# A decoder step on one core: the prompt group's final retention state computed and stored in the routing stretch instead of among the branch projections

## The chip, the core and the metric

One Trainium2 core runs the whole program. The metric is device time in microseconds (us) of one execution. The kernel before took 1251.85, 1258.98 and 1262.05 us in three runs, median 1258.98 us. One execution was also profiled, and its trace is what this document reads.

## What is computed

264 tokens (256 of a prompt, 8 decode samples) go through one layer: an input projection, three token mixers (a recurrent branch, a retention branch, cross attention to memory), a gated merge, an output projection, and then a mixture of 32 experts with a router. The change touches one output of the retention branch alone, the state that the prompt leaves behind (`ret_p`, 4 heads x 256 x 512, 2 MB in float32):

```
def step(s, inp):                       # retention, per chunk and head
    qc, kc, vc = inp
    att = einsum('bhnk,bhmk->bhnm', qc, kc) * dmask
    o = einsum('bhnm,bhmv->bhnv', att, vc) + einsum('bhnk,bhkv->bhnv', qc * q_decay, s)
    s = s * s_decay + einsum('bhmk,bhmv->bhkv', kc * k_decay, vc)
    return s, o
s_last, o = lax.scan(step, s0, chunks)  # s_last of the prompt group is ret_p
...
grp_logits = x @ w_grp + b_grp          # router: top group, then 2 of its 8 experts
y = sum over experts of (silu(x @ w_gate) * (x @ w_up) * weight) @ w_down
```

For the prompt, which starts from a zero state, `s_last` is one product per head, decayed keys transposed times values over all 256 positions. Nothing later in the layer reads it: it only has to be stored.

## The kernel before

Activations lie transposed, channels on the 128 partitions and the 264 tokens along the free axis. All engines follow one list of tasks that `tensor_order` writes out (line 250 on), each taking from it the tasks it has a part in, in that order. TensorE (PE) makes a product into one of eight PSUM banks, ScalarE (ACT) or VectorE (DVE) takes it out. Projections (`ga`, `gc`, `lru_out`, `mem_out`, ...: 128 output channels each, 8 products of 128x128 by 128x264) turn over banks 0 to 3, side tasks over banks 4 to 6. PE waits at a task for its bank (`begin`), the evicting engine for the product (`full`).

**The branch stretch.** `tensor_order` weaves 32 projections with the prompt's retention tasks `ret` (per head: `att`, four `o`, and two `S`) and with the tasks of the 16 half states of the samples (`sd`, `so`: 8 samples x 2 pairs of heads, 1 MB each, in a ring of three buffers `st`). A half state goes through four engines: POOL loads it (line 895), ACT decays it in two halves (`sd`, copies of 128x1024 with a scale), DVE adds key times value (`sd`, line 1654, four instructions), PE reads it with the query (`so`, line 1193), and POOL stores it (line 920). POOL's loop per half state is: wait for the update, store, copy a row of values to partition 0 with a small DMA (line 901), wait for that, broadcast the row (line 905), load the half state after next. Task `S` is what the change moves: `("S", h, i)` is two products of 128x128 by 128x512 (line 1181, `k_rows` and `v_rows`), a copy by ACT into one of two buffers `S_st`, and a 256 KB store to `ret_p` issued from ACT's queue (line 1376). ACT waits for the store before last before it fills a buffer again.

**After it** come the last projections (`gb`, `g`, `ret_out`, `x2`) and the normed residual, which ends the list.

**The routing stretch.** `router_products` (line 605 on) has PE make the router's logits (line 609), transpose the tokens back to rows in six steps u = 0 to 5 (line 618; u = 4 and 5 are the last 8 tokens), and, when DVE has the expert masks, the ranks of the tokens (lines 631 to 634). ACT copies each step's rows out in two forms and then a middle part (loop at 1411 to 1427), POOL makes the remainders. Behind the copies of u = 2 ACT waits for DVE (`router_exp_in`) and takes an exponential that DVE waits for. DVE picks groups and experts in a chain of small instructions up to the masks (line 1770), then waits for the ranks. `gather(0, 0)` (line 648) starts the expert loop on PE: 16 pairs of experts, whose weights SP streams, 12 MB a pair. SP's queue in this stretch holds the weights of expert 1 (line 795), four parts of the last expert that have a buffer of their own (`last_gate_up`, line 798), and then the loop's loads, each waiting until PE is through with the buffer (line 809).

Buffers are placed by lifetimes in stages (`BUFFERS`: size, first stage, last stage).

Of the kernel before, what the change touches and what calls it, by code (L numbers as in the profile page):

```python
# [33 lines left out]
P = 128  # L34
D = 1024
# [27 lines left out]
def shape_constants():  # L63
# [85 lines left out]
    "vT": (VT * T, "v", "rows"),  # L149
    "v_rows": (2 * HEADS * DV, "rows", "gc"),  # L150
    "k_rows": (2 * D, "v", "gc"),
    "vs_rows": (HEADS * DV, "rows", "gc"),
# [8 lines left out]
    "oT": (VT * T, "ga", "ret"),  # L161
    "S_st": (2 * DV, "ga", "gb"),
    "os": (DV, "ga", "gb"),
# [6 lines left out]
    "rbias": (NLOG, "load", "end"),  # L170
    "last_gate_up": (4 * CHUNK, "x2", "end"),
    "filler": (24, "route", "end"),
# [76 lines left out]
def tensor_order():  # L249
# [29 lines left out]
    for h in heads:  # L279
        ret += [("att", h)] + [("o", h, j) for j in range(4)] + [("S", h, i) for i in range(2)]  # L280

# [51 lines left out]
def build_program(nc, dram, outs, const_at):  # L333
# [55 lines left out]
    with ExitStack() as ctx:  # L389
# [156 lines left out]
        st_decayed, st_updated, st_read = sem("st_decayed"), sem("st_updated"), sem("st_read")  # L546
        s_out = [sem("s_out_0"), sem("s_out_1")]
        o_normed, g_tanh, ret_ready = sem("o_normed"), sem("g_tanh"), sem("ret_ready")
        branch_merged = sem("branch_merged")
# [20 lines left out]
        def states_stored(eng):  # L570

            for i in range(3):
                eng.wait_ge(st_out[i], 16 * len(range(i, 2 * NS, 3)))
            for i in range(2):
                eng.wait_ge(s_out[i], 16 * HEADS)

# [26 lines left out]


        def router_products(pe):

# [4 lines left out]
            for u in range(2 * TT):  # L611
                t, k4 = divmod(u, 2)
                n = min(P, T - t * P)
                if u >= 2:

                    pe.wait_ge(row_high, u - 1)
                for k in range(4):
                    mm = pe.transpose(psum[0:n, u % 2, k * P:(k + 1) * P], xnT[:, 4 * k4 + k, t * P:t * P + n], ident)
                mm.then_inc(row_full, 1)
                if u == 1:  # L620
                    pe.wait_ge(logitsT_ready, 1)
                    for s in range(TT):
                        m = min(P, T - s * P)
                        mm = pe.transpose(psum[0:m, 2, s * 64:s * 64 + NLOG], lgT[0:NLOG, s * P:s * P + m],
                                          ident[0:NLOG, 0:NLOG])
                    mm.then_inc(logits_full, 1)
            pe.wait_ge(masks_ready, 1)
            pe.wait_ge(tables_set, 2)
# [114 lines left out]
        def _(sp):  # L743
# [48 lines left out]
            for i in range(6):  # L792
                if i < RING1:
                    full(sp, last_task[max(n for n in range(NCH) if n % RING1 == i)])
                sp.dma_start(into(i, i), expert_part(1, i)).then_inc(chunk_loaded[i], 16)

            for i in range(4):
                sp.dma_start(last_gate_up[:, i, :].rearrange("p (k n) -> p k n", k=4),
# [30 lines left out]
            for q in range(4):  # L829
                sp.wait_ge(final_normed, 2 * q + 2)  # L830
                sp.dma_start(outs["y"].rearrange("(k p) n -> p k n", p=P)[:, 2 * q:2 * q + 2],
                             y_out[:, 2 * q:2 * q + 2]).then_inc(stored, 16)
            sp.wait_ge(stored, 16 * 4)
            sp.nop()
# [126 lines left out]
        def _(pe):  # L961
# [56 lines left out]
            for task in order:  # L1018
# [146 lines left out]
                elif kind == "o":  # L1165
                    _, h, j = task
                    if j == 0:
# [6 lines left out]
                                        start=False, stop=True))  # L1174
                elif kind == "S":
                    _, h, i = task
                    if i == 0:
                        read(pe, ("kr", 1, 1))
                    begin(task)
                    for m in range(2):  # L1180
                        mm = pe.matmul(ps(task)[:, 0:DV], k_rows[:, m, (2 * h + i) * P:(2 * h + i + 1) * P],  # L1181
                                       v_rows[:, m, h * DV:(h + 1) * DV], start=m == 0, stop=m == 1)
                    end(task, mm)
                elif kind == "so":
# [51 lines left out]
        def _(act):  # L1236
# [12 lines left out]
            for task in order:  # L1249
# [114 lines left out]
                elif kind == "o":  # L1364
                    _, h, j = task
                    full(act, task)
                    run(oT[:, 4 * h + j, 0:TP], ps(task)[:, 0:TP], ACT.Copy, free_of(task))
                elif kind == "S":
                    _, h, i = task
                    n = 2 * h + i  # L1370
                    full(act, task)
                    if n >= 2:
                        act.wait_ge(s_out[n % 2], 16 * (n // 2))
                    run(S_st[:, n % 2, :], ps(task), ACT.Copy, free_of(task))
                    steps.settle()
                    act.dma_start(outs["ret_p"][h, i * P:(i + 1) * P, :], S_st[:, n % 2, :]).then_inc(s_out[n % 2], 16)
                elif kind == "oq":
# [29 lines left out]
            def rows_of(u):  # L1407
                t, k4 = divmod(u, 2)
                return min(P, T - t * P), t, slice(512 * k4, 512 * k4 + 512)

            for u in range(2 * TT + 1):
                if u < 2 * TT:
# [12 lines left out]
                if u == 2:  # L1425
                    act.wait_ge(router_exp_in, 1)
                    run(tmpB[:, 0:TT * 8], tmpB[:, 0:TT * 8], ACT.Exp, router_exp)

            def take_tokens(g, half):
# [47 lines left out]
        def _(dve):  # L1477
# [17 lines left out]
            for task in order:  # L1495
# [100 lines left out]
                elif kind in ("rot_q", "rot_k"):  # L1596
# [5 lines left out]

                    full(dve, ("i", KT - 1))
                    v(V.tensor_tensor(t1, x2_, sin, ALU.mult))
# [9 lines left out]
                elif kind == "sl":  # L1614

                    full(dve, ("i", KT - 1))
                    v(V.memset(buf("PM"), 0.0))
# [303 lines left out]
```

## Time and profile before

| | |
|---|---|
| three runs | 1251.85, 1258.98, 1262.05 us |
| span of the profiled execution | 1255.6 us |
| busy PE / DVE / ACT / POOL | 1185.2 / 385.5 / 237.3 / 100.3 us |
| share of the chain that ended last, by engine | PE 89%, DVE 6%, ACT 2%, DMA 1% |
| branch stretch, `sd`/`so` tasks | 335 to 508 us |
| routing stretch, last `x2` product to first gather | 685 to 722 us |
| expert pairs | 722 to 1243 us |

Times in rows are us from the start of the span. "L1181" is line 1181 of the kernel before. ACT's evictions all carry L1240, the line of a helper, so they are told apart by shape and time. A float32 product counts as two instructions of PE. The granted TensorE clock (PEclk) stands as a share of full speed: 1.00 is 2.4 GHz, 0.50 is 1.2 GHz.

### The profile page before, as it was taken

Reading aid. Unit: us, or ns where it says so; the run is one execution under the profiler, and the core shown is the slowest. Engines: PE = TensorE matmul, PEld = TensorE weight load, DVE = VectorE, ACT = ScalarE, POOL = GpSimd, SP = SyncE. Lnnn points to the kernel's source line nnn. Section 1 sums busy time; section 2 is a strip of 40 time slices with the busy share of each in tenths; the row PEclk is TensorE's granted clock in tenths of the full one; section 3 lists DMA queues with packets and bytes.
Section 4 is the critical chain, followed back from the end, with each engine's and each line's share of the span. In section 5 each row is a group of like instructions: output and inputs, shape, how many; then the busy total and the mean of one; then the engine's idle time right before and its main releaser. Section 6 shows DMA issues by size and latency. Waiting matters only on the chain.

```text
span 1255.6 us, 18012 instructions
## 1 busy us (share of the span) xinstructions
PE 1185.2 (94%) x7398; PEld 776.4 (62%) x7398; DVE 385.5 (31%) x696; ACT 237.3 (19%) x449; POOL 100.3 (8%) x127
## 2 busy tenths in 40 slices
PE   6999999999889999999998399999999999999996
PEld 5888888778666766888887154444444444444442
DVE  1203572385323334232111752222211222222222
ACT  2112124123422222321001311111111111111112
POOL 0001120000332322000000400000000000000000
PEclk9999999999999999999999689999999999999999
DMA  8774566675688889335356738999999999999981
GB/s 282 241 256 143 171 210 225 195 244 136 215 273 310 293 279 307 127 126 185 103 167 241 292 135 313 394 394 394 394 394 395 394 394 394 394 394 394 394 310 37
DMA packets 187948, 343.36 MB, mean 273 GB/s; under 512 B 7640, under 2 KB 91864, under 8 KB 187896
## 3 DMA queue, kind: packets, MB, share of 16 engines
q1 hardware_dynamic: 172288, 287.95, 64.2%
q0 software_dynamic: 14464, 52.68, 12.2%
q10 hardware_dynamic: 1152, 2.10, 0.4%
q8 instruction: 33, 0.54, 0.2%
q14 instruction: 11, 0.09, 0.0%
HBM read 320.47 MB, written 22.20 MB: 273 GB/s over the span
## 4 chain that ended last, share of the span: by engine, by line
PE 89%; DVE 6%; ACT 2%; DMA 1%; issue 1%; POOL 0%; DVEq 0%; ACTq 0%
PE psum L988 35%; PE psum L686 18%; PE psum L710 9%; PE psum L648 6%; PE psum L1038 4%; PE psum L723 4%; PE psum L1193 2%; PE psum L997 2%; ACT arena L1240 2%; DVE arena L1808 2%; PE psum L1007 1%; PE psum L1181 1%; DVE arena L1553 1%; DMA arena<-arena 1%; PE psum L1132 1%
## 5 line engine op out<-in xcount | busy, mean ns | idle before, releaser
L988 PE MATMUL psum<-arena 128*128 128x264 f32 x2048 | 473.4, 388 | 0.0
L988 PEld LDWEIGHTS psum<-arena 128*128 128x128 f32 x2048 | 386.1, 190 | 82.2 <-issue 18.6
L1240 ACT ACTIVATE arena<-psum 128x256 f32<-128x256 f32 (+3 forms) x276 | 117.9, 442 | 632.4 <-PE psum L988 263.2
L686 PE MATMUL psum<-arena 128*64 128x512 f32 x1024 | 228.9, 598 | 0.9 <-ACT arena L1240 0.9
L686 PEld LDWEIGHTS psum<-arena 128*64 128x64 f32 x1024 | 73.4, 138 | 141.7 <-issue 141.6
L710 PE MATMUL psum<-arena 128*64 128x512 f32 x512 | 113.4, 595 | 11.1 <-ACT arena L1240 11.1
L1801 DVE SCALAR_TENSOR_TENSOR arena<-arena,psum 128x256 f32<-128x256 f32 x32 | 13.5, 422 | 346.4 <-ACT arena L1240 346.4
L648 PEld LDWEIGHTS psum<-arena 128*128 128x128 bf16 x2304 | 70.7, 99 | 28.0 <-issue 28.0
L1654 DVE SCALAR_TENSOR_TENSOR arena<-arena 128x512 f32<-128x512 f32 x64 | 54.8, 916 | 105.5 <-ACT arena L1240 90.4
L1240 ACT ACTIVATE arena<-arena 128x1024 f32<-128x1024 f32 (+7 forms) x67 | 58.7, 903 | 150.6 <-DVE arena L1694 84.8
L710 PEld LDWEIGHTS psum<-arena 128*64 128x64 f32 x512 | 35.3, 137 | 78.9 <-issue 64.0
L723 PE MATMUL psum<-arena 128*128 128x264 f32 x272 | 78.4, 411 | 5.2 <-ACT arena L1455 1.3
L648 PE MATMUL psum<-arena 128*128 128x64 bf16 x2304 | 74.5, 195 | 2.7 <-DVE arena L1795 2.7
L1808 DVE TENSOR_TENSOR arena<-arena,psum 128x264 f32<-128x264 f32 x136 | 58.3, 429 | 52.5 <-PE psum L723 51.4
L723 PEld LDWEIGHTS psum<-arena 128*128 128x128 f32 x272 | 42.0, 188 | 35.8 <-DVE arena L1808 25.2
L1038 PE MATMUL psum<-arena 128*128 128x256 f32 x256 | 56.3, 379 | 3.1 <-DVE arena L1501 3.1
L1038 PEld LDWEIGHTS psum<-arena 128*128 128x128 f32 x256 | 48.2, 190 | 9.8 <-issue 3.4
L1455 ACT ACTIVATE arena<-psum 128x1024 f32<-128x1024 f32 x16 | 16.4, 1024 | 115.9 <-PE psum L710 115.9
L1193 PE MATMUL psum<-arena 128*8 128x512 f32 x128 | 30.2, 593 | 3.2 <-DVE arena L1654 3.2
L905 POOL PARTITION_BROADCAST arena<-arena x16 | 21.8, 1360 | 106.6 <-DMA arena<-arena 106.6
L997 PE MATMUL psum<-arena 128*128 128x264 f32 x128 | 29.8, 386 | 0.0
L997 PEld LDWEIGHTS psum<-arena 128*128 128x128 f32 x128 | 24.3, 190 | 4.2
(233 smaller groups left out, 641.5 us busy)
## 6 DMA issues: line engine op xcount, KB each, us to landing
arena<-in_w_gate SPq DMA_DIRECT2D x64, 1024.0 KB, 13.5
arena<-in_w_up SPq DMA_DIRECT2D x64, 1024.0 KB, 14.1
arena<-in_w_down SPq DMA_DIRECT2D x64, 1024.0 KB, 12.8
arena<-in_w_in SPq DMA_DIRECT2D x48, 1024.0 KB, 5.3
arena<-in_state_ret POOLq DMA_DIRECT2D x16, 1024.0 KB, 6.8
out_ret_s<-arena POOLq DMA_DIRECT2D x16, 1024.0 KB, 7.6
arena<-in_w_mem_kv SPq DMA_DIRECT2D x8, 1024.0 KB, 9.5
arena<-in_cache_mem_k POOLq DMA_DIRECT2D x8, 1024.0 KB, 5.9
```

The lines of the kernel that those rows point to most:

```text
L648: mm = pe.matmul(psum[:, 0, k * SLOTS:(k + 1) * SLOTS], xr[x][:, t, k * P:(k + 1) * P], Sb[:, t, half * SLOTS:(half + 1) * SLOTS], start=t ...
L686: mm = pe.matmul(psum[64 * a:64 * a + SLOTS, 2, :], XgT[:, half, k, :], w[:, :, 256 * a:256 * a + 256], start=k == 0, stop=k == KT - 1)
L710: mm = pe.matmul(psum[64 * half:64 * half + SLOTS, 4 + dh, :], hT[:, half, f % 2, f // 2, :], w[:, f % 2, dh * 512:(dh + 1) * 512], start= ...
L723: pe.matmul(psum[:, 6 + d % 2, 0:T], yS[:, d * P:(d + 1) * P], SwT, start=True, stop=True).then_inc(scatter_full, 1)
L905: nc.gpsimd.partition_broadcast(vb[:, s % 2, :], v_row0[0:1, :], P).then_inc(v_bcast, 1)
L988: mm = pe.matmul(ps(task)[:, 0:T], w[:, k, (i % 2) * P:(i % 2 + 1) * P], rhs[:, k, :], start=k == 0, stop=k == KT - 1 and not two)
L997: mm = pe.matmul(ps(task)[:, 0:T], w[:, k, (i % 2) * P:(i % 2 + 1) * P], rhs[:, KT + k, :], start=False, stop=k == KT - 1)
L1038: mm = pe.matmul(ps(task)[:, 0:256], memT[:, k, m * P:(m + 1) * P], w[:, k, :], start=k == 0, stop=k == KT - 1)
L1193: mm = pe.matmul(psum[32 * h:32 * h + NS, 7, :], QM[:, 2 * h + i, b, :], st[:, s % 3, 2 * h2 + i, :], start=b == 0 and i == 0, stop=b == N ...
L1240: steps.did(nc.scalar.activation(out, in_, func, **kw), sem)
L1654: did(V.scalar_tensor_tensor(x, vb[:, s % 2, h2 * DV:(h2 + 1) * DV], kT[:, 2 * (2 * hp + h2) + i, TP + b:TP + b + 1], x, ALU.mult, ALU.add ...
L1808: V.tensor_tensor(x_res[:, d, :], x_res[:, d, :], psum[:, 6 + d % 2, 0:T], ALU.add).then_inc(scatter_added, 1)
```

## The change

Task `S` leaves the woven list. Its products become `state_products`, called from `router_products` behind the transposes of u = 2 (state 0), 3 (state 1), 4 (states 2 and 3) and 5 (states 4 to 7), into banks 4 and 5. Its copies and stores become `stage_states`, called in ACT's loop over u at u = 3 (state 0), 4 (1), 5 (2 and 3) and 6 (4 to 7). PE waits at state n for the copy of state n - 2, ACT from state 2 on for the store of state n - 2. `k_rows` and `v_rows` now live until the routing stretch, `last_gate_up` only from the expert loop on, and SP loads it when all eight products are done. The waits on all of `ret_p`'s stores go to the end of SP's program. At two places DVE waits for ACT's eviction of the last `i` gate where it waited for PE's product.

```diff
-    "v_rows": (2 * HEADS * DV, "rows", "gc"),
-    "k_rows": (2 * D, "v", "gc"),
+    "v_rows": (2 * HEADS * DV, "rows", "route"),
+    "k_rows": (2 * D, "v", "route"),
...
-    "S_st": (2 * DV, "ga", "gb"),
+    "S_st": (2 * DV, "route", "route"),
...
-    "last_gate_up": (4 * CHUNK, "x2", "end"),
+    "last_gate_up": (4 * CHUNK, "moe", "end"),
...
-        ret += [("att", h)] + [("o", h, j) for j in range(4)] + [("S", h, i) for i in range(2)]
+        ret += [("att", h)] + [("o", h, j) for j in range(4)]
...
-            for i in range(2):
-                eng.wait_ge(s_out[i], 16 * HEADS)
...
+        def state_products(pe, states):
+            for n in states:
+                h, i = divmod(n, 2)
+                if n == 0:
+                    read(pe, ("kr", 1, 1))
+                if n >= 2:
+                    pe.wait_ge(s_staged, n - 1)
+                for m in range(2):
+                    mm = pe.matmul(psum[:, 4 + n % 2, :], k_rows[:, m, (2 * h + i) * P:(2 * h + i + 1) * P],
+                                   v_rows[:, m, h * DV:(h + 1) * DV], start=m == 0, stop=m == 1)
+                mm.then_inc(s_full, 1)
...
                     mm.then_inc(logits_full, 1)
+                if u >= 2:
+                    state_products(pe, ((), (), (0,), (1,), (2, 3), (4, 5, 6, 7))[u])
             pe.wait_ge(masks_ready, 1)
...
+            sp.wait_ge(s_full, 2 * HEADS)
             for i in range(4):
                 sp.dma_start(last_gate_up[:, i, :].rearrange("p (k n) -> p k n", k=4),
...
+            for i in range(2):
+                sp.wait_ge(s_out[i], 16 * HEADS)
             sp.wait_ge(stored, 16 * 4)
...
-                elif kind == "S":
-                    _, h, i = task
-                    n = 2 * h + i
-                    full(act, task)
-                    if n >= 2:
-                        act.wait_ge(s_out[n % 2], 16 * (n // 2))
-                    run(S_st[:, n % 2, :], ps(task), ACT.Copy, free_of(task))
-                    steps.settle()
-                    act.dma_start(outs["ret_p"][h, i * P:(i + 1) * P, :], S_st[:, n % 2, :]).then_inc(s_out[n % 2], 16)
...
+            def stage_states(states):
+                for n in states:
+                    h, i = divmod(n, 2)
+                    act.wait_ge(s_full, n + 1)
+                    if n >= 2:
+                        act.wait_ge(s_out[n % 2], 16 * (n // 2))
+                    run(S_st[:, n % 2, :], psum[:, 4 + n % 2, :], ACT.Copy, s_staged)
+                    act.wait_ge(s_staged, n + 1)
+                    act.dma_start(outs["ret_p"][h, i * P:(i + 1) * P, :], S_st[:, n % 2, :]).then_inc(s_out[n % 2], 16)
...
+                if u >= 3:
+                    stage_states(((0,), (1,), (2, 3), (4, 5, 6, 7))[u - 3])
...
-                    full(dve, ("i", KT - 1))
+                    read(dve, ("i", KT - 1))
```

The end of the branch stretch on PE, before. L1181 is task `S`, L1193 `so`, L988 a projection, L1172 and L1173 task `o`; the last L1193 reads half state 15.

```order
L1193 MATMUL psum<-arena 8x512 x4
L988 MATMUL psum<-arena 128x264 x8
L1172 MATMUL psum<-arena 128x256
L1173 MATMUL psum<-arena 128x128
L988 MATMUL psum<-arena 128x264 x8
L1181 MATMUL psum<-arena 128x512 x2
L1193 MATMUL psum<-arena 8x512 x4
L988 MATMUL psum<-arena 128x264 x8
L1181 MATMUL psum<-arena 128x512 x2
L1193 MATMUL psum<-arena 8x512 x4
L988 MATMUL psum<-arena 128x264 x16
```

The same place with the change. `so` is L1201, a projection L1005, task `o` L1189 and L1190.

```order
L1201 MATMUL psum<-arena 8x512 x4
L1005 MATMUL psum<-arena 128x264 x8
L1189 MATMUL psum<-arena 128x256
L1190 MATMUL psum<-arena 128x128
L1005 MATMUL psum<-arena 128x264 x8
L1201 MATMUL psum<-arena 8x512 x4
L1005 MATMUL psum<-arena 128x264 x8
L1189 MATMUL psum<-arena 128x256
L1190 MATMUL psum<-arena 128x128
L1201 MATMUL psum<-arena 8x512 x4
L1005 MATMUL psum<-arena 128x264 x16
```

The two `S` are gone; between the last two `so` stand one projection and one `o`.

PE in the routing stretch with the change, from the transposes of u = 4 (first row) to the ranks (last row). L613 is a state product; each waits for a copy by ACT (`s_staged`).

```order
L630 MATMUL psum<-arena 8x128 [waits row_high]
L630 MATMUL psum<-arena 8x128 x3
L613 MATMUL psum<-arena 128x512 [waits s_staged]
L613 MATMUL psum<-arena 128x512
L613 MATMUL psum<-arena 128x512 [waits s_staged]
L613 MATMUL psum<-arena 128x512
L630 MATMUL psum<-arena 8x128 [waits row_high]
L630 MATMUL psum<-arena 8x128 x3
L613 MATMUL psum<-arena 128x512 [waits s_staged]
L613 MATMUL psum<-arena 128x512
...
L646 MATMUL psum<-arena 128x32 [waits tables_set,masks_ready]
```

Before, the L613 rows were not there: the ranks stood directly behind the eight transposes of u = 4 and 5. Three more states (5 to 7) stand where the line of dots is.

ACT in the same stretch with the change, from the exponential to the copy of state 2. The rows of 8x512 are the row copies of u = 4 and u = 5.

```order
L1248 ACTIVATE arena<-arena 128x24 [waits router_exp_in]
L1248 ACTIVATE arena<-psum 128x512 [waits row_rest,row_full]
L1248 ACTIVATE arena<-psum 128x512
L1248 ACTIVATE arena<-arena 128x512 [waits row_rest]
L1248 ACTIVATE arena<-psum 128x512 [waits s_full]
L1419 DMA out_ret_p<-arena 128x512 [waits s_staged]
L1248 ACTIVATE arena<-psum 8x512 [waits row_rest,rows_zero,row_full]
...
L1248 ACTIVATE arena<-psum 8x512 [waits row_rest,row_full]
L1248 ACTIVATE arena<-psum 8x512
L1248 ACTIVATE arena<-arena 8x512 [waits row_rest]
L1248 ACTIVATE arena<-psum 128x512 [waits s_out_0,s_full]
```

Before, the rows that wait for `s_full` and the stores (L1419) were not there. State 0 is copied behind the exponential, and state 2 behind the row copies of u = 5, which wait for PE's transposes (`row_full`).

## Rows read from the trace of the kernel before

**Rows 1.** The page: span.
```profile
span 1255.6 us, 18012 instructions
```

**Rows 2.** Busy time by stretch: PE, PEld, DVE, ACT, POOL, PEclk, DMA share, GB/s.
```profile
335.00:508.00 173.00, 169.33 (x731) 117.94 (x730) 63.23 (x87) 42.81 (x65) 47.84 (x58) 0.99 0.82 278
...
697.00:722.00 25.00, 5.01 (x41) 3.04 (x41) 21.60 (x54) 10.85 (x20) 14.79 (x17) 0.63 0.71 268
```

**Rows 3.** Chain that ended last, end of the branch stretch: start, us, what.
```profile
497.30 1.72 PE psum L1181 x4
499.02 1.82 PE psum L1193 x8
```

**Rows 4.** Waits of PE, ACT and POOL, 335 to 510: us in total, times, longest.
```profile
PE psum L1172 <- DVE arena L1644: 3.7, 1, 3.7
...
ACT arena L1240 <- DMA arena<-in_state_ret: 52.2, 13, 8.9
...
POOL arena L905 <- DMA arena<-arena: 97.7, 15, 8.5
POOL out_ret_s L920 <- DVE arena L1654: 19.8, 10, 7.6
```

**Rows 5.** Timeline, POOL: first and last of 13 state loads: start, us, instruction.
```profile
350.68 0.82 POOL L895 DMA_DIRECT2D arena<-in_state_ret  x1
...
486.57 0.80 POOL L895 DMA_DIRECT2D arena<-in_state_ret  x1
```

**Rows 6.** Timeline: decay and update of half state 15 [idle before, releaser].
```profile
492.22 2.00 ACT L1240 ACTIVATE arena<-arena 128x1024 f32<-128x1024 f32 x2 [5.36 <-DMA arena<-in_state_ret]
...
494.37 2.74 DVE L1654 SCALAR_TENSOR_TENSOR arena<-arena 128x512 f32<-128x512 f32 x4 [4.83 <-ACT arena L1240]
```

**Rows 7.** DMA, 335 to 510 (packets, MB, share; issues); last row whole span.
```profile
q10 hardware_dynamic: 1152, 2.10, 3.1%
...
out_ret_p<-arena ACTq DMA_DIRECT2D x8, 256.0 KB, 4.8
...
out_y<-arena SPq DMA_DIRECT2D x4, 264.0 KB, 2.2
```

**Rows 8.** Timeline, ACT: copy and store of one state in the branch stretch.
```profile
350.98 0.60 ACT L1240 ACTIVATE arena<-psum 128x512 f32<-128x512 f32 x1 [1.32 <-PE psum L1181]
351.61 0.40 ACTq L1376 DMA_DIRECT2D out_ret_p<-arena  x1
```

**Rows 9.** Timeline of the routing stretch: u = 3 and 5, and the ranks.
```profile
709.20 1.07 ACT L1240 ACTIVATE arena<-psum 128x512 f32<-128x512 f32 x2
...
710.15 0.63 ACT L1240 ACTIVATE arena<-arena 128x512 bf16<-128x512 f32 x1
...
710.32 1.02 PE L618 MATMUL psum<-arena 128*8 128x128 f32 x4 [6.85 <-ACT arena L1240]
...
718.67 0.21 PE L632 MATMUL psum<-arena 128*128 128x32 bf16 x1 [7.34 <-DVE arena L1770]
```

**Rows 10.** Busy time in steps of 5 us, columns as in Rows 2.
```profile
705.00:710.00 5.00, 0.00 (x0) 0.00 (x0) 3.99 (x20) 0.93 (x3) 0.85 (x1) 0.50 1.05 387
...
715.00:720.00 5.00, 0.42 (x9) 0.32 (x9) 4.65 (x11) 0.63 (x1) 4.66 (x9) 0.50 0.00 0
```

**Rows 11.** Chain that ended last, first expert pair: gathers and gate-up products.
```profile
721.83 4.01 PE psum L648 x72
...
726.71 9.03 PE psum L686 x32
735.74 2.21 PE psum L648 x72
...
743.36 7.02 PE psum L686 x32
```

**Rows 12.** Timeline, SP: the expert loop's first load.
```profile
732.49 0.39 SPq L809 DMA_DIRECT2D arena<-in_w_gate  x1
```

**Rows 13.** Timeline, DVE: first instruction that needs the gate bank's successor (task `sl`).
```profile
220.43 0.41 DVE L1621 TENSOR_REDUCE arena<-psum 32x1 f32<-32x256 f32 x1 [2.49 <-PE psum L1114]
```

More of the change, by code:

```diff
@@ L547, in build_program @@
         s_out = [sem("s_out_0"), sem("s_out_1")]
+        s_full, s_staged = sem("s_full"), sem("s_staged")
         o_normed, g_tanh, ret_ready = sem("o_normed"), sem("g_tanh"), sem("ret_ready")
@@ L1174, in _ @@
                                         start=False, stop=True))
-                elif kind == "S":
-                    _, h, i = task
[L1177 to L1183, printed above, removed]
                 elif kind == "so":
@@ L1367, in _ @@
                     run(oT[:, 4 * h + j, 0:TP], ps(task)[:, 0:TP], ACT.Copy, free_of(task))
-                elif kind == "S":
-                    _, h, i = task
-                    n = 2 * h + i
-                    full(act, task)
-                    if n >= 2:
-                        act.wait_ge(s_out[n % 2], 16 * (n // 2))
-                    run(S_st[:, n % 2, :], ps(task), ACT.Copy, free_of(task))
-                    steps.settle()
-                    act.dma_start(outs["ret_p"][h, i * P:(i + 1) * P, :], S_st[:, n % 2, :]).then_inc(s_out[n % 2], 16)
                 elif kind == "oq":
@@ L1614, in _ @@
                 elif kind == "sl":
-                    full(dve, ("i", KT - 1))
+                    read(dve, ("i", KT - 1))
                     v(V.memset(buf("PM"), 0.0))
```

## Prediction

> **What bounds the kernel now.** I read the shares of the chain first: PE is 89% of it, so whatever leaves PE looks like a gain. The question is stretch by stretch whether PE's work there, or something PE is about to wait for, ends last.
>
> In the branch stretch PE is busy 169.3 of 173 us at a granted clock of 0.99 [rows 2], and it stands still once, 3.7 us [rows 4]. That reads as bound by PE. But a second chain runs beside it, the 16 half states of the samples, and the waits say that it does not depend on PE: ACT waits 13 times for a half state to land, POOL 15 times for the small row DMA (97.7 us) and 10 times for DVE's update (19.8 us), and neither POOL nor DVE's updates wait for PE [rows 4]. POOL issues the last 13 loads from 350.68 to 486.57 us, one in 11.3 us [rows 5]. The last half state is decayed as it lands (492.22) and its update ends at 494.37 + 2.74 = 497.1 [rows 6]; PE reads it at 499.02, right behind the last `S` [rows 3]. So at the end of this stretch PE is only 1.9 us behind the state chain. Two bounds lie almost on each other.
>
> In the routing stretch PE works 5 of 25 us, with the clock at 0.63 [rows 2]. There DVE's mask chain sets the end: PE waits 7.34 us for it before the ranks at 718.67 [rows 9], and the gather follows at 721.83 [rows 11]. ACT works 10.85 of the 25 us and POOL 14.79 [rows 2].
>
> **The change part by part.**
>
> *Removed from the branch stretch:* 8 tasks `S`, 16 products. A pair takes 1.72 us on PE at full clock [rows 3], together 13.8 us. Each also takes a copy of 0.60 us and a store issue of 0.40 us on ACT [rows 8], 8 us, which lie in ACT's waiting time. What PE gains it loses again waiting for the half states: without `S`, PE is ready for the last `so` some 12 us early, but the update still ends at 497.1. The last `so` therefore starts at about 497.2 instead of 499.02: 1.8 us. Two order rows show what is left between the last two `so`, one projection and one `o`, which is not enough to make PE late again.
>
> The state chain itself may get a little faster, since the stores to `ret_p` leave the DMA engines: they took 3.1% of the 16 engines' time in this window [rows 7], 5.4 us. Nothing of it is gained if the chain's waits are for its own transfers, all of it if every store stood in the chain's way. The row DMA stands behind a store and beside a load of 1 MB each on its own queue, against which 256 KB are small; I take 1.5 us. Branch stretch: -3.3 us (-1.8 to -7.2).
>
> *The 3.7 us stall* at an `o` is on PE alone. With the change more such stalls come, up to some 12 us in all; they cost nothing as long as the state chain ends last.
>
> *Added to the routing stretch.* On PE 8 pairs, chained with ACT's copies by `s_staged`, and ACT's copies chained with the stores from state 2 on. All of PE's part stands ahead of the ranks in PE's order. I follow it in the times of the trace.
> - States 0 and 1 go behind the transposes of u = 2 and 3, before ACT's exponential; PE waits there anyway. Free.
> - ACT copies state 0 only behind the exponential and the work of u = 3: copies from 709.20 (1.07), middle part (0.63, from 710.15) [rows 9], copy 0.60 [rows 8]: 711.3. Only then may PE start state 2.
> - PE has idled for 6.85 us at that time, and the clock stands at 0.50 from 705 on [rows 10]: a pair takes 3.44 us instead of 1.72. States 2 and 3: 711.3 + 6.9 = 718.2 (state 1 is copied at 713.7, in time). The transposes of u = 5, which in the kernel before ran at 710.32, follow: 1.02 us [rows 9], 719.2.
> - ACT is waiting for those: copies 1.07, middle part 0.63, copy of state 2 0.60: 721.5. Store issue 0.40, copy of state 3: 722.5.
> - PE, states 4 and 5: I take full clock. In the first pair PE began at 721.83, and its 9.03 us of gate-up products are 4.0 us at half and 5.0 at full clock if 7.02 is the whole at full clock [rows 11], so the clock rose at about 730.7, behind 8.9 us of work; here PE has by 721.5 worked for 10 us with one gap. 721.5 + 3.4 = 724.9.
> - State 4 is copied when the store of state 2 has landed. A 264 KB store into idle engines took 2.2 us [rows 7], and here they are idle, at share 0.00 from 715 to 720 [rows 10]: 723.7, copied 724.3; state 5, with its product at 724.9: 725.5.
> - States 6 and 7: 724.9 to 728.4. The ranks follow there instead of at 718.67: +9.7 us.
>
> What is queued behind: on PE the ranks, for which DVE waits with the slots, and so the gather and all 16 pairs; on ACT only the copy of the first gather, later than the copy of state 7; on SP `last_gate_up` and the loop's first load.
>
> Bounds: all pairs at full clock, state 2 on, moves everything from u = 5 on 3.3 us earlier: +6.4. All at half clock: 721.5 + 4 x 3.44 = 735.3, +16.6. Stores as slow as in the branch stretch, 4.8 us [rows 7]: states 4 and 5 copied at 726.9 and 727.9, last product at 730.3, +11.6.
>
> The Trainium skill ("DMA: Bandwidth & Descriptors", section "Issuing engines are not separate DMA queues") says that transfers issued by ACT run on the same 16 engines as those of SP and interleave with them; weights under way here would give the +11.6. The trace speaks for idle engines, as the row of 715 to 720 shows.
>
> *Given back.* In the kernel before the first gather and the first gate-up products come on a cold PE: 4.01 and 9.03 us against 2.21 and 7.02 in the next half pair [rows 11]. If the state products keep the clock up across the 3 us from ranks to gather, 3.8 us come back; if it falls again, none. I take half, 1.9. Routing stretch: +7.8 us (+2.6 to +16.6).
>
> *`last_gate_up` later.* Four loads of 1 MB at 387 GB/s [rows 10] are 10.8 us. They leave when all products are done, 3.4 us before the gather; the loop's first load comes 10.7 us behind the gather [rows 11, 12], so there are 14 us for them. Cost 0; without that cover, up to 10.8.
>
> *The two waits on the gate's eviction, and the lifetimes:* DVE's two memsets start one eviction later, under 1 us, and DVE idles 2.49 us behind them before the next instruction, for PE [rows 13]. Cost 0. The waits at the end cost 0, the stores are over 500 us old.
>
> **Sum.** -3.3 + 7.8 = +4.5 us. The profiled span is 1255.6 [rows 1]; the median of the runs, 1259.0, lies 3.4 us above, within the spread of the three. I add the change to the median: 1263.5 us.
>
> **The rivals.**
> 1. *The clock stays at 0.50 throughout the routing stretch* (slower). PE's pairs come in bursts between waits for ACT. Then +16.6, nothing given back, and with the smallest branch gain, -1.8, the sum is +14.8: 1273.8. For it: the rows of 705 to 720 stand at 0.50. Against it: from 711.3 on PE has work with gaps of some 2 us only. It decides from the third state on: pairs of states 4 to 7 at 3.4 us instead of 1.7. The Trainium skill ("TensorE: Matmul & The Clock Gate", section "Part 1: The HAM clock gate") calls the throttled clock the default that activity releases. By it work moved from a busy stretch into an idle one costs double, which speaks against this change; the two levels stand in the rows, 0.99 in the branch stretch and 0.50 here. Chance 0.15.
> 2. *The branch stretch really is bound by PE* and gives all 13.8 us: -13.8 + 7.8 = -6.0, 1253.0; with the cheapest routing stretch (+2.6) -11.2, 1247.8. For it: PE's busy share. Against it: POOL, ACT and DVE show no wait for PE in the state chain. It would need half states at 10.5 us apiece instead of 11.3. Chance 0.12.
> 3. *`last_gate_up` pushes the loop's loads* and the first pairs wait for weights: up to 10.8 us on top of +4.5, 1274.3. Against it: the 14 us of cover. Chance 0.05.
> 4. My forecast, 1254.4 (-7.2 + 2.6) to 1268.8 (-1.8 + 11.6): chance 0.68.
>
> **Range and chances.** From 1251 to 1274: it leaves out the better part of rival 2 and the worst of rivals 1 and 3. A measurement of this kernel tells about 1%, 12.6 us, from no change. Slower by over 1% is most of rival 1, part of rival 3 and the tip of the forecast with a bad draw: 0.17. Faster by over 1% is rival 2 at its best: 0.05. Within 1%: 0.78.
>
> **What would show it.** Right: the last `so` starts only 2 to 7 us earlier, and PE now waits for DVE's updates at most `so`; the state loads still come every 11 us; PE waits for ACT's copies at the state products from state 2 on; the ranks come 8 to 12 us later after the last `x2`; the first gather takes nearer 2.2 than 4.0 us. Wrong: branch stretch shorter by over 8 us; the state products done before DVE's masks; weights late in pair 1; or states 4 to 7 on a half clock.

## The result, and the profile after

Over 20 runs of each kernel the median went from 1259.53 to 1268.87 us. The ratio is 1.0057, with a 95% interval from 1.0032 to 1.0082: the change costs 7.2 us (4.0 to 10.3). (The medians lie 9.3 us apart; the ratio leaves out runs over 1.5% above the fastest of their kernel.) It is a small loss, but the interval leaves no doubt of its sign, which the forecast of +4.5 us had right.

The profiled execution of the changed kernel spans 1265.1 us, against 1255.6 [rows 1]. A second execution of each was profiled later, with no edit, because the first pair differs in two places and one of them turned out to be chance. They are called "again" below. Times are from the start of the span; the last column is the span less the column before it.

| | last state updated | first router product | exponential | ranks | second gate-up | span | rest |
|---|---|---|---|---|---|---|---|
| before | 497.1 | 690.47 | 709.07 | 718.67 | 743.29 | 1255.6 | 512.3 |
| before again | 497.9 | 689.74 | 706.51 | 716.11 | 740.92 | 1253.4 | 512.5 |
| after | 504.0 | 695.54 | 712.38 | 732.18 | 752.82 | 1265.1 | 512.3 |
| after again | 497.5 | 690.59 | 707.70 | 725.37 | 747.39 | 1259.6 | 512.2 |

Three things can be read here. Behind the second gate-up products nothing changed. From the exponential on, the changed kernel is 6.2 us longer in the first pair (40.44 against 34.22) and 5.3 us in the second (39.69 against 34.41). The end of the branch stretch is 7 us later in the first pair and as good as equal in the second.

**The branch stretch.** Busy time of the changed kernel, columns as in [rows 2]:

```profile
335.00:508.00 173.00, 155.15 (x674) 109.00 (x674) 58.58 (x85) 37.67 (x57) 48.86 (x58) 0.94 0.78 261
```

PE's busy time in this window fell from 169.33 [rows 2] to 155.15 us, by about the 13.8 us of the eight `S`. The stretch got no shorter for it. PE now stands still for 17.9 us instead of 3.7, and the waits from 335 to 510 us (total, times, longest) say for whom:

```profile
POOL arena L922 <- DMA arena<-arena: 106.5, 15, 9.4
ACT arena L1248 <- DMA arena<-in_state_ret: 101.6, 13, 12.1
...
PE psum L1189 <- DVE arena L1656: 11.6, 2, 5.9
...
PE psum L1201 <- DVE arena L1666: 6.3, 2, 4.9
```

POOL still waits 15 times for its small row DMA, and ACT 13 times for a half state, now 101.6 instead of 52.2 us [rows 4]. Decay, update and query of half state 15, in the timeline (start, duration, instruction, idle before and releaser):

```profile
499.09 2.00 ACT L1248 ACTIVATE arena<-arena 128x1024 f32<-128x1024 f32 x2 [5.79 <-DMA arena<-in_state_ret]
...
501.23 2.74 DVE L1666 SCALAR_TENSOR_TENSOR arena<-arena 128x512 f32<-128x512 f32 x4 [6.47 <-ACT arena L1248]
...
504.03 1.89 PE L1201 MATMUL psum<-arena 128*8 128x512 f32 x8 [1.36 <-DVE arena L1666]
```

Here the order is plain: the state lands, ACT, DVE, and PE takes it 0.06 us after the update ends. Before, the last `so` came 1.9 us after it, behind an `S` [rows 3, 6]. In after again PE came to the last `so` at 499.07, 1.6 us behind the update and without a wait: there it had lost its time earlier, 13.9 us over the stretch.

**The routing stretch.** The same view of the changed kernel:

```profile
695.54 5.44 PE L621 MATMUL psum<-arena 128*36 128x264 f32 x16 [3.51 <-DVE arena L1713]
...
712.38 0.22 ACT L1248 ACTIVATE arena<-arena 128x24 f32<-128x24 f32 x1 [2.70 <-DVE arena L1767]
...
714.63 6.37 PE L613 MATMUL psum<-arena 128*128 128x512 f32 x8 [6.12 <-ACT arena L1248]
720.84 0.60 PE L630 MATMUL psum<-arena 128*8 128x128 f32 x4
...
723.59 8.75 PE L613 MATMUL psum<-arena 128*128 128x512 f32 x16 [2.15 <-ACT arena L1248]
...
727.23 0.60 ACT L1248 ACTIVATE arena<-psum 128x512 f32<-128x512 f32 x1 [1.58 <-PE psum L613]
...
732.18 0.18 PE L646 MATMUL psum<-arena 128*128 128x32 bf16 x1
732.37 0.37 SPq L813 DMA_DIRECT2D arena<-in_w_gate  x1
...
734.98 2.26 PE L662 MATMUL psum<-arena 128*128 128x64 bf16 x72 [2.42 <-DVE arena L1807]
738.12 7.09 PE L700 MATMUL psum<-arena 128*64 128x512 f32 x32 [0.88 <-ACT arena L1248]
```

PE idles 6.12 us until ACT, behind the exponential, has copied state 0. Then states 2 and 3 take 6.37 us where 3.44 would do at full clock, PE waits 2.15 us for ACT again, and states 4 to 7 take 8.75 us. The ranks no longer wait for DVE's masks, as they did for 7.34 us [rows 9]: they have no bracket, PE simply gets to them last. In return the first gather takes 2.26 and its gate-up products 7.09 us, where it was 4.01 and 9.03 [rows 11].

The clock in this place (columns as in [rows 2]):

```profile
710.00:715.00 5.00, 0.37 (x1) 0.37 (x2) 4.16 (x15) 2.20 (x5) 2.24 (x3) 0.50 0.00 0
715.00:720.00 5.00, 5.00 (x7) 1.90 (x7) 4.65 (x11) 2.06 (x4) 3.17 (x3) 0.50 0.28 105
720.00:725.00 5.00, 2.85 (x9) 1.36 (x8) 0.27 (x2) 2.65 (x5) 2.25 (x2) 0.84 0.11 44
725.00:730.00 5.00, 5.00 (x10) 2.00 (x9) 0.00 (x0) 1.82 (x3) 2.40 (x6) 0.81 0.30 113
```

From 715 to 720 PE is busy all the time and is granted 0.50, 1.2 GHz: the engine had idled for 6.12 us just before. In the kernel before PE did 0.42 us of work there [rows 10]. In the last two rows the clock is at 1.00 from 720 on, falls to 0.50 once more at the start of states 4 to 7, behind the pause of 2.15 us (hence the means of 0.84 and 0.81), and stands at 1.00 from 727 on, the gather included. In after again it stayed at 1.00 across that same pause, so that states 4 to 7 took 7.13 us, and fell in the pause ahead of the gather, which took 3.71 us.

### The profile page after: what moved, and what is told of

Its sections match the earlier page's. It is cut to its first block, busy times and chain, and to the rows that moved or that the text cites. A ratio compares the mean times of both kernels' runs of the same rounds, so it can differ in the third digit from the quotient of the medians.

```text
span 1265.1 us, 18004 instructions
## 1 busy us (share of the span) xinstructions
PE 1189.0 (94%) x7398; PEld 777.4 (61%) x7398; DVE 378.6 (30%) x696; ACT 236.5 (19%) x449; POOL 101.9 (8%) x127
## 4 chain that ended last, share of the span: by engine, by line
PE 76%; DVE 7%; issue 6%; DMA 4%; ACT 3%; POOL 2%; DVEq 0%; POOLq 0%; ACTq 0%
PE psum L1005 26%; PE psum L700 17%; PE psum L724 9%; PE psum L662 5%; PE psum L1055 4%; PE psum L737 4%; ACT arena L1248 3%; DMA arena<-in_state_ret 3%; PE psum L1014 2%; DVE arena L1820 2%; DVE arena L1666 1%; DMA arena<-arena 1%; PE psum L1024 1%; POOL arena L922 1%; PE psum L613 1%
## 5 line engine op out<-in xcount | busy, mean ns | idle before, releaser
L1005 PE MATMUL psum<-arena 128*128 128x264 f32 x2048 | 473.9, 388 | 0.0
L1005 PEld LDWEIGHTS psum<-arena 128*128 128x128 f32 x2048 | 387.1, 191 | 82.1 <-issue 18.0
L1248 ACT ACTIVATE arena<-psum 128x256 f32<-128x256 f32 (+4 forms) x276 | 117.4, 441 | 596.4 <-PE psum L1005 244.3
L1248 ACT ACTIVATE arena<-arena 128x1024 f32<-128x1024 f32 (+7 forms) x67 | 58.7, 903 | 197.4 <-DMA arena<-in_state_ret 101.6
L1666 DVE SCALAR_TENSOR_TENSOR arena<-arena 128x512 f32<-128x512 f32 x64 | 51.1, 859 | 122.1 <-ACT arena L1248 107.4
L1820 DVE TENSOR_TENSOR arena<-arena,psum 128x264 f32<-128x264 f32 x136 | 58.2, 429 | 51.2 <-PE psum L737 50.1
L737 PEld LDWEIGHTS psum<-arena 128*128 128x128 f32 x272 | 42.1, 188 | 35.9 <-DVE arena L1820 26.4
L1201 PE MATMUL psum<-arena 128*8 128x512 f32 x128 | 32.8, 637 | 9.6 <-DVE arena L1666 9.6
## 6 DMA issues: line engine op xcount, KB each, us to landing
arena<-in_w_up SPq DMA_DIRECT2D x64, 1024.0 KB, 14.1
```

Of the source, the lines that this page charges most:

```text
L737: pe.matmul(psum[:, 6 + d % 2, 0:T], yS[:, d * P:(d + 1) * P], SwT, start=True, stop=True).then_inc(scatter_full, 1)
L1005: mm = pe.matmul(ps(task)[:, 0:T], w[:, k, (i % 2) * P:(i % 2 + 1) * P], rhs[:, k, :], start=k == 0, stop=k == KT - 1 and not two)
L1201: mm = pe.matmul(psum[32 * h:32 * h + NS, 7, :], QM[:, 2 * h + i, b, :], st[:, s % 3, 2 * h2 + i, :], start=b == 0 and i == 0, stop=b == N ...
L1248: steps.did(nc.scalar.activation(out, in_, func, **kw), sem)
L1666: did(V.scalar_tensor_tensor(x, vb[:, s % 2, h2 * DV:(h2 + 1) * DV], kT[:, 2 * (2 * hp + h2) + i, TP + b:TP + b + 1], x, ALU.mult, ALU.add ...
L1820: V.tensor_tensor(x_res[:, d, :], x_res[:, d, :], psum[:, 6 + d % 2, 0:T], ALU.add).then_inc(scatter_added, 1)
```

## The experiments

Each ratio is against runs of the kernel before on the same chip. The theory: in the branch stretch the chain of half states ends last, so `S` is free there; in the routing stretch the states' products and copies, chained between PE and ACT, delay the ranks. The rivals: PE bounds the branch stretch; the products alone, or the clock, make the routing stretch dear.

**1. No `S` at all** (`ret_p` is not computed or stored; compared with the kernel before).

```diff
-        ret += [("att", h)] + [("o", h, j) for j in range(4)] + [("S", h, i) for i in range(2)]
+        ret += [("att", h)] + [("o", h, j) for j in range(4)]
...
-            for i in range(2):
-                eng.wait_ge(s_out[i], 16 * HEADS)
```

> The kernel before with task S left out altogether (ret_p is not computed, 8 pairs of products, 8 copies and 8 stores fewer, nothing put in their place). It measures what the branch stretch gives back when S leaves. Theory A, the half states' chain (load, decay, update, store, row DMA) ends that stretch: within -3 to +4 us of the kernel before, although 13.8 us of products at full clock are gone, and PE waits for DVE's updates at most `so`. Rival, PE bounds the stretch: -13.8 us, ratio about 0.989.

1261.44 against 1258.14 us, ratio 1.0001 (0.9967 to 1.0035, which is -4.2 to +4.4 us). 13.8 us of PE's work, eight copies and eight stores less make no difference. That PE alone bounds the branch stretch is excluded; so is a relief of the state chain through the missing stores of more than some 4 us. The waits of this kernel in the branch stretch show where the time went:

```profile
POOL arena L903 <- DMA arena<-arena: 109.7, 15, 10.6
...
PE psum L1191 <- DVE arena L1652: 9.0, 4, 3.5
...
PE psum L1170 <- DVE arena L1642: 7.9, 2, 5.1
```

PE waits for DVE at four of the sixteen `so` (L1191), not at most of them as expected, and at two `o` (L1170), and POOL for its row DMA no less than before.

**2. The same load on PE in the routing stretch, tied to nothing** (the kernel before with eight pairs of products of the same shape, on data that lies there anyway, no copies and no stores).

```diff
                     mm.then_inc(logits_full, 1)
+                if u >= 3:
+                    for n in range((2, 2, 4)[u - 3]):
+                        for m in range(2):
+                            pe.matmul(psum[:, 4 + n % 2, :], ident, buf("x")[:, 512 * m:512 * m + 512],
+                                      start=m == 0, stop=m == 1)
```

> The kernel before with 8 pairs of 128x128 by 128x512 products added on PE in the routing stretch, behind the transposes of u = 3 (2), 4 (2) and 5 (4), read by nobody and waiting for nobody. It measures the clock term alone: products there without copies and stores. If they end before the masks (718.7 us) and keep the clock at 2.4 GHz, the first gather falls from 4.0 to 2.2 us and the first gate-up products from 9.0 to 7.0: -3.8 us in all. If the products run at 1.2 GHz throughout, the last four end some 5 us behind the masks and the sum is +1 to +5 us.

1259.18 us, ratio 0.9995 (0.9962 to 1.0028). From the first router product to the ranks 26.2 us, as in before again (26.4). So PE's work alone costs nothing that could be measured in this place (-4.8 to +3.5 us). The timeline, from the last four pairs on:

```profile
724.19 7.03 PE L630 MATMUL psum<-arena 128*128 128x512 f32 x16
...
732.12 0.19 PE L637 MATMUL psum<-arena 128*128 128x32 bf16 x1 [0.90 <-DVE arena L1775]
...
735.28 3.34 PE L653 MATMUL psum<-arena 128*128 128x64 bf16 x72 [2.77 <-DVE arena L1800]
739.50 8.77 PE L691 MATMUL psum<-arena 128*64 128x512 f32 x32 [0.88 <-ACT arena L1245]
```

The four pairs ran at full clock (7.03 us), PE then waited 0.90 us for the masks instead of 7.3, and still the gather and the gate-up products were slow. The expected gain of 3.8 us came to about 1 in this trace (23.7 us from the ranks to the second gate-up, against 24.6 and 24.8 before). A warm PE at the ranks does not secure the clock behind them.

**3. Both kernels again, profiled only.**

> The changed kernel once more, for a second execution's trace. If the state chain of the branch stretch ended late in the first trace (update of half state 15 at 504.0 us against 497.1 before) because of the change, it is again at 502 to 506 here; if that was one execution's draw of DMA times, it lies anywhere from 495 to 506. The routing stretch is the same to within 1 us: ranks 42 us behind the last x2 product.

> The kernel before once more, for a second execution's trace: if the end of its state chain (497.1 us in the first) is a draw, it moves by several us here; if it is set by the program, it is within 1 us.

1261.24 and 1255.22 us. The numbers stand in the table above. In after again the last update came at 497.5, which by the expectation makes the 504.0 a draw. In before again it moved by 0.8 us only, which by itself would have said that the program sets it; experiment 2 says otherwise. The ranks came 42.0 us behind the last `x2` products in after and 40.2 in after again, so the routing stretch was not the same to within 1 us. The update of half state 15 in after again, in before again, and in experiment 2, whose branch stretch is the program of before:

```profile
494.72 2.74 DVE L1666 SCALAR_TENSOR_TENSOR arena<-arena 128x512 f32<-128x512 f32 x4 [4.26 <-ACT arena L1248]
```
```profile
495.13 2.74 DVE L1654 SCALAR_TENSOR_TENSOR arena<-arena 128x512 f32<-128x512 f32 x4 [5.09 <-ACT arena L1240]
```
```profile
506.95 2.74 DVE L1659 SCALAR_TENSOR_TENSOR arena<-arena 128x512 f32<-128x512 f32 x4 [4.73 <-ACT arena L1245]
```

With `S` in the stretch the last update ended at 497.1, 497.9 and 509.7 us, without it at 504.0, 497.5, 504.7 (experiment 1) and 502.3 (experiment 6). The spread from execution to execution, 12 us, is larger than the 7 us of the first pair, which must not be read as the effect of the change.

**4. Before, with POOL's row DMA issued ahead of the store.** In the kernel before POOL stores a half state and only then fetches the next row of values, on the same queue. Here the row (and the load of a half state) goes first:

```diff
                 b, hp = n_state(s)
+                if s + 2 < 2 * NS:
+                    v_row(s + 2)
+                    if s >= 1:
+                        load_state(s + 2)
                 pool.wait_ge(st_updated, s + 1)
...
                 if s + 2 < 2 * NS:
-                    v_broadcast(s + 2)
-                    if s >= 1:
-                        load_state(s + 2)
+                    v_spread(s + 2)
```

> The kernel before with another order in POOL's loop over the half states: row DMA and next load are issued ahead of the wait for the update and of the store, and the broadcast comes behind the store. Theory A (half states and PE bound the branch stretch almost equally before): the state chain gets shorter, but PE's work including S then bounds alone, so only the stall at one `o` and the last wait go: 0 to -6 us, and the last update ends well ahead of the last `so`. If the chain were bound by DMA bandwidth and not by the order, nothing changes.

1252.07 against 1260.61 us, ratio 0.9931 (0.9906 to 0.9955): 8.7 us (5.7 to 11.9), more than the 0 to 6 expected. The expectation counted the 3.7 us for which PE stood still in one execution; in before again it was 0.9, and in experiment 2, whose branch stretch is the same program, 14.1. The waits and the busy time of the branch stretch in this kernel:

```profile
POOL arena L895 <- DMA out_ret_s<-arena: 92.6, 13, 9.3
...
POOL arena L911 <- DMA arena<-arena: 4.9, 2, 4.1
```
```profile
335.00:508.00 173.00, 172.73 (x754) 120.82 (x752) 54.66 (x91) 44.71 (x69) 51.11 (x58) 1.00 0.86 280
```

The wait for the row fell from 97.7 [rows 4] to 4.9 us. POOL now waits for a store to leave the buffer that the next load needs, and the chain is faster all the same. The row itself lands no sooner. The DMA issues in the kernel before and in this one (KB each, median us from issue to landing):

```profile
arena<-arena POOLq DMA_DIRECT2D x14, 4.0 KB, 7.5
```
```profile
arena<-arena POOLq DMA_DIRECT2D x14, 4.0 KB, 7.7
```

So the new order does not shorten the row's way, it hides it: the row is under way while POOL waits for something else. PE is busy 172.73 of 173 us: with the shorter state chain PE does bound this stretch, and the last `so`, at 494.40, is late by 2.9 us behind its update (488.73 + 2.74).

**5. The change on top of that.** The same edit of POOL's loop in the changed kernel.

> The changed kernel with the same new order in POOL's loop. Theory A: with the state chain out of the way S leaving PE is worth up to its 13.8 us in the branch stretch, and only the routing cost of some 6 us stays: against the kernel with the new order and S in the branch stretch -5 to -10 us, against the kernel before -5 to -14 us. Rival (the branch stretch gains nothing from S leaving for another reason than the state chain): slower than that kernel by about 6 us.

1250.01 us, ratio 0.9912 (0.9879 to 0.9946). Timeline:

```profile
483.16 1.89 PE L1209 MATMUL psum<-arena 128*8 128x512 f32 x8 [1.08 <-DVE arena L1674]
...
674.68 6.32 PE L621 MATMUL psum<-arena 128*36 128x264 f32 x16 [3.52 <-DVE arena L1721]
```

The last `so` starts 11.2 us earlier than in experiment 4 (494.40) and the first router product too (674.68 against 685.92). So most of the 13.8 us can be had there, once PE is the bound. The routing stretch takes 7.1 us of it back: from the first router product to the second gate-up 58.4 us against 51.25. By the spans (1249.1 and 1245.5 us) 3.6 us remain, by the ratios 0.0019, 2.4 us, with intervals that overlap. The direction is as expected, the size below the 5 to 10 us expected.

**6. The changed kernel with the coupling between PE and ACT loosened.** Four buffers and four banks for the states instead of two, most of the products one step earlier, and ACT's first four copies ahead of the exponential:

```diff
-                if n >= 2:
-                    pe.wait_ge(s_staged, n - 1)
+                if n >= 4:
+                    pe.wait_ge(s_staged, n - 3)
...
-                    state_products(pe, ((), (), (0,), (1,), (2, 3), (4, 5, 6, 7))[u])
+                    state_products(pe, ((), (), (0, 1), (2, 3), (4, 5), (6, 7))[u])
...
                 if u == 2:
+                    stage_states((0, 1, 2, 3))
                     act.wait_ge(router_exp_in, 1)
...
-                if u >= 3:
-                    stage_states(((0,), (1,), (2, 3), (4, 5, 6, 7))[u - 3])
+                if u >= 4:
+                    stage_states(((4, 5), (), (6, 7))[u - 4])
```

> The changed kernel with the routing stretch's chain loosened: states 0 to 3 are copied by ACT ahead of the exponential, four banks and four staging buffers instead of two each, products 0,1 / 2,3 / 4,5 / 6,7 behind u = 2 / 3 / 4 / 5. Theory: the 9 us by which the ranks came late were PE and ACT waiting for each other behind the exponential; products then end before the masks and the ranks are 26 to 29 us behind the first router product, as in the kernel before, so the sum is within -3 to +2 us of the kernel before. If what costs is the work itself on PE at 1.2 GHz or on ACT, the ranks stay over 32 us behind.

1264.11 against 1260.61 us, ratio 1.0018 (0.9988 to 1.0047). PE's timeline:

```profile
695.56 6.31 PE L621 MATMUL psum<-arena 128*36 128x264 f32 x16 [3.52 <-DVE arena L1714]
...
715.74 3.60 PE L613 MATMUL psum<-arena 128*128 128x512 f32 x8
722.61 0.19 PE L646 MATMUL psum<-arena 128*128 128x32 bf16 x1 [3.27 <-DVE arena L1783]
...
726.66 4.00 PE L662 MATMUL psum<-arena 128*128 128x64 bf16 x72 [3.66 <-DVE arena L1808]
731.54 8.74 PE L700 MATMUL psum<-arena 128*64 128x512 f32 x32 [0.88 <-ACT arena L1248]
```

The products run four at a time at full clock (3.60 us for two states), the last ones end 3.3 us ahead of the masks, and the ranks come 27.05 us behind the first router product: 28.2 and 26.4 before, 36.6 and 34.8 with the change. So it is not the work that delays the ranks, but its coupling to copies behind the exponential. Buffers, products and copies were changed together; which of the three did most is not separated. By the whole time it is +2.3 us (-1.5 to +5.9), an interval that overlaps that of the change. The gather is back at 4.00 and the gate-up products at 8.74 us, though PE worked until 719; to the second gate-up it is 52.3 us, against 52.8 and 51.2 before.

**7. Both edits on the changed kernel.**

> Both together: new order in POOL's loop and the loosened routing stretch. If both theories hold, the branch stretch gives up to 13.8 us and the routing stretch costs nothing: -8 to -18 us against the kernel before, faster than either alone.

1244.29 us, ratio 0.9877 (0.9836 to 0.9917): 15.5 us faster than the kernel before, and the fastest of all, in six runs. The last `so` stands at 486.62, 7.8 us earlier than in experiment 4, the second gate-up comes 52.9 us behind the first router product. The gain over experiment 4, which keeps `S` where it was, is 0.0054, 6.8 us; the two intervals just overlap. That is the best figure here for what moving the states is worth when the state chain does not end last and the ranks are not delayed.

## Why the prediction was right, and where it was not

**The branch stretch, -3.3 us: mechanism right, size wrong.** That the state chain ends last there, and that PE would lose by waiting what it gained, is shown by experiment 1 (13.8 us less work, ratio 1.0001) and from the other side by experiments 4 and 5 (a faster state chain, and the same 13.8 us bring 11.2 at the last `so`; 7.8 in experiment 7). The two bounds do lie almost on each other: in before again PE was busy for 172.1 of the 173 us. The two terms that made the -3.3 failed. The -1.8, the last `so` straight behind the update, took the update's end at 497.1 as given; it moves by several us between executions of one program. In after the `so` did follow within 0.06 us, of an update that came 7 us later. The forecast sign, a last `so` 2 to 7 us earlier, did not appear: it starts at 504.03 and 499.07, against 499.02 [rows 3] and 498.22. The -1.5, relief by the missing stores, was estimated from a share of 3.1% of the DMA engines' time [rows 7]; POOL's wait for the row was 97.7, 98.4 and (experiment 2) 108.6 us with those stores and 106.5, 97.6, 109.7 and 103.8 without: no relief to be seen. Measured: about 0.

**Where PE waits.** Forecast: for DVE's update at most of the sixteen `so`. Seen: twice at an `o` (11.6 us) and twice at a `so` (6.3). In order, PE stops at whichever task meets DVE late; the new stops come to 14.2 us, the forecast said up to some 12; in after again all stops come to 13.9. They also cost clock: its mean over the stretch fell from 0.99 to 0.94, and the `so` at 377.75 took 3.59 us where the last one takes 1.89.

**The routing stretch, +7.8 us: measured +5.3 to +6.2.** The way there was the one described, though two of the working's small sums are off by 0.1 to 0.2 us (711.3 is 711.4 by its own rows, and the bound at full clock is 3.5 us earlier, +6.3, not 3.3 and +6.4). State 2 starts 2.25 us behind the exponential (forecast 711.3 - 709.07 = 2.23), its pair and the next run at half clock (6.37 us; forecast 6.9), ACT makes PE wait again (2.15). From the start of state 2 to the ranks it is 17.55 us, where the working gave 17.1. Two details differ. States 4 to 7 started at half clock and took 8.75 us instead of 6.9; in after again and in experiment 5 they took 7.13. And ACT's copies of states 4 on wait for PE's products (1.58 us before the copy at 727.23), not for the stores. From the exponential to the ranks: 9.60 us in both traces of before, 19.80, 17.67 and 18.15 (experiment 5) with the change: +8.1 to +10.2, forecast +9.7.

**Given back, -1.9 us: measured -4.0 and -2.8** (ranks to second gate-up, 24.6 and 24.8 before, 20.6 and 22.0 after). Taking half was too little for these two traces. In experiment 5 against 4 it is 22.1 and 24.9. Part of the -4.0 is only the clock's cost in another place: it fell once more in each trace, ahead of state 4 in after (1.6 us more there than in after again) and ahead of the gather in after again (1.5 us more there). In the three traces in which the state products run straight up to the ranks, the first gate-up products took 7.09 us; where PE waited for the masks ahead of the ranks (0.90 to 7.34 us) they took 8.74 to 9.28, but in experiment 1, without any state products, 7.09 too. What decides is not settled. Part of the difference may be chance.

**`last_gate_up`: 0, as forecast.** Its first load is issued at 732.37 us, and the second gate-up products take 7.09 us with no wait for weights; behind them the rest is 512.3 us in both kernels. The cover was shorter than the 14 us reckoned: the loop's first load came at 741.96, 9.6 us behind, less than the 10.8 us worked out for the four loads. It cost nothing all the same.

**The sum.** About 0 and +5.3 to +6.2, against -3.3 and +7.8. Two errors of some 3 and 2 us partly cancelled, which is luck, so that +4.5 is 2.7 us below the measured 7.2, inside its interval; the 1263.5 us lie 5.4 below the median of 20 runs. Of the measured 7.2 us the routing stretch explains 5 to 6. The remaining 1 to 2 us would lie in the branch stretch, where PE's stops might slow the chain a little; the interval does not separate them from 0, and no run shows it.

**The rivals.** That the branch stretch is bound by PE fell with experiment 1. That the clock stays at 0.50 throughout came true for states 2 and 3 and, in the first trace only and after a rise between them, for the beginning of 4 to 7, no further: the last two ran fast and the gather took 2.26 us. The Trainium skill ("TensorE: Matmul & The Clock Gate", section "Part 1: The HAM clock gate") calls the throttled clock the state from which activity releases PE. The trace agrees for the first products behind the pause of 6.12 us, with their 6.37 us. That weights come late in the first pairs did not occur.

## What to carry to other kernels

Work taken from an engine that is 98% busy was worth nothing here, because a second chain ends beside it; look for an engine whose waits never name the busy one, and shorten that chain first (here by one reordered issue, 0.7%), after which the same move paid about 6.8 us. Work moved into idle time can still cost if it ties two engines together in order: products alone cost nothing measurable there, products that wait for copies queued behind another engine's wait made the ranks 8 to 10 us late, 5 to 6 us in all. Before reading a difference out of a pair of traces, profile each kernel twice and compare from a common event, here the exponential.

## What the hardware showed that was not expected

A small DMA, one row of 4 KB, took 7.5 us (median) from issue to landing on the queue that also carries the loads and stores of 1 MB, and kept POOL waiting up to 10.7 us (15 waits, 97.6 to 109.7 us in all). Issued ahead of the next store it took 7.7 us and landed no sooner, but POOL had two waits for it of together 4.9 us. Whether the 1 MB transfers are what makes it slow was not tested. The end of the chain of half states differed by up to 12 us between executions of one program (497.1 and 509.7). On the chip of experiments 4 to 7 the kernel before ran from 1254.06 to 1269.44 us, over 15 us; with the shorter chain of experiment 4 the runs lie within 8 us (1247.85 to 1255.57). That fits a spread that comes from the state chain, but was not tested by itself. Whether TensorE keeps its clock across a pause of some 2.5 us differs between executions: behind a pause of 2.42 us the first gather took 2.26 us in after and 3.71 in after again.
